# Layer 1's twelve modulation chunks as products on VectorE in dense blocks 0 to 6, identity products in their place in the second attention

## The chip, the cores and the metric

The kernel runs on one core of a Trainium2 chip. The metric is the device time of one execution in microseconds (us). Three runs of the kernel before took 1367.85, 1368.5 and 1369.38 us; the median is 1368.5 us.

## The reference, cut to what matters

A trunk of two layers works on 256 tokens of width 1024, in f32. Each layer takes six modulation vectors of 1024 numbers from a conditioning vector `c`, and uses them around an attention and around a feed-forward part: dense in layer 0, eight experts (two per token) in layer 1.

```python
c_act = silu(c)
for layer in range(2):
    mod = c_act @ ada_w[layer] + ada_b[layer]        # 1024 x 6144 weights, one row
    sh_m, sc_m, g_m, sh_f, sc_f, g_f = split(mod, 6)
    h = rms_norm(x, norm_mix_g[layer]) * (1 + sc_m) + sh_m
    x = x + g_m * token_mixer(h, ...)                # in-projection, attention, out-projection
    h = rms_norm(x, norm_ffn_g[layer]) * (1 + sc_f) + sh_f
    y = swiglu(h, ...) if layer % 2 == 0 else moe_swiglu(h, ...)
    x = x + g_f * y
return rms_norm(x, final_g)
```

The change touches only `c_act @ ada_w[1]`, a vector times a 25 MB matrix, and when and on which engine it is done.

## The kernel before, in words

**Stages.** In order of time: a lead-in with layer 0's first modulation chunks, layer 0's in-projection, first attention and out-projection, the dense feed-forward in seven blocks of 512 hidden columns (`dense`, blocks 0 to 6), layer 1's in-projection, second attention and out-projection, the router, and the experts (352 MB of weights). Each engine runs its own hand-written instruction list, tied together by semaphores. Nothing is reordered at run time.

**Weights.** SP issues nearly all weight DMAs, in one in-order queue. Up to the second out-projection weights land in five slots of 2 MB: slots 0, 1 and 2 of `W`, and two spare ones. ScalarE copies a weight slot to a rounded high part (L1010), VectorE subtracts to get the low part (L1328), and PE multiplies high by high, low by high and high by low (L2256 to L2258). A slot is free once both splits are done. A dense block takes slot 0 and 1 for gate and up weights (parts 0 to 3) and slot 2 for down weights (parts 4 and 5).

**Modulation.** `ada_w` of a layer is cut into twelve chunks of 2 MB. Four chunks (`n // 4`, a round) give 2048 of the 6144 numbers; each holds a quarter of the 1024 rows of the sum. There are two ways to work one off:

- On PE (`ada_chunk`, L2178): eight products of the conditioning column `c_rep` with 512 columns, four of them side by side in four column groups.
- On VectorE (`products`, L1653 and L1655): weight slot times a column of `vcols`, added to `ada_acc` (128 x 2048), two instructions per chunk, after which `ada_summed` is raised. The first instruction of a round overwrites `ada_acc` and is shorter. When four chunks are in, PE adds over partitions with four products by ones (`sum_rows`, L2422) and raises `ada_rows`. VectorE then adds the bias (`mod_round`, L1392).

Before, layer 0's chunks all go through PE. Of layer 1's, chunks 0 to 7 go through VectorE in dense blocks 1 to 4, two per block (`ADA_BLOCKS`): slot 1's in `before_last_units`, slot 2's in `after`. Their loads go into the weight slots between two blocks' weights, so the next block's weights for that slot wait for `ada_summed`. Chunks 8 to 11 go through PE in the second attention, one in each of its first four steps, from slots 1, 2 and the spare ones. The sums of rounds 0 and 1 stand behind the last product of blocks 2 and 4.

**Experts.** 18 buffers of 1 MB (`raw`), in pairs r = 0 to 8, lie over the memory of earlier stages, and `first_free(r)` says what must have ended before a pair is first filled: for r = 0, 1, 3 and 5 the modulation chunks 8 to 11, for the others parts of the out-projection. Later fills wait for PE to finish with what the buffer held.

The prediction also names `turned` (VectorE's low part of transposed activations, L1640), `gated` (gate times up, L1635), `turn` (PE's transposes of activations, L2388), `dense_out` (gated residual addition, L1937) and `keep` (products of the identity with itself that nobody reads, L2186).

## Time and profile before

| what | us |
|---|---|
| median of three runs | 1368.5 |
| the profiled execution, its own time | 1368.58 |
| its span on the core | 1366.8 |
| PE busy | 1296.5 |
| VectorE (DVE) busy | 452.3 |
| ScalarE (ACT) busy | 290.5 |

Dense block 0 begins at about 161 us, the in-projection of layer 1 at about 398, the second attention at 456.9 and the first expert's products at 541.25. From then to the end the experts' weights stream in.

How to read the rows: a row of a timeline has the start, the duration, engine, line, operation, output and inputs, shape and count; in brackets stands how long the engine had been idle and who ended it. A row of windows has the stretch, its length, the busy time of PE, PEld (weight load), DVE, ACT and POOL with counts, TensorE's granted clock (1.00 is 2.4 GHz, 0.50 is 1.2 GHz), the busy share of the DMA engines and GB/s. A row of the chain has start, duration, engine and line. PE shows two rows' worth of records for one f32 product of the attention, `ada_chunk`, `sum_rows` and `keep` (x8 is four products).

### The profile page before, as it was taken

What the parts mean: (1) busy time and instruction counts of PE and PEld (TensorE: products, weight loads), DVE (VectorE), ACT (ScalarE), POOL (GpSimd) and SP (SyncE); (2) the same over time, 40 slices, a digit from 0 to 9 for tenths busy, and PEclk for the clock granted to TensorE, in tenths of its full rate; (3) what the DMA queues carried; (4) which work ended last, traced back from release to release, by engine and by line L of the source; (5) the groups of instructions that cost most, each with busy time, mean ns of one, the idle gap of its engine ahead of it and who ended that gap; (6) DMA issues with size and microseconds to landing.
All of it is one profiled execution on the core that took longest, in us unless ns stands there. A gap on an engine that the chain in (4) does not pass through costs nothing.

```text
span 1366.8 us, 24966 instructions
## 1 busy us (share of the span) xinstructions
PE 1296.5 (95%) x10994; PEld 704.0 (52%) x10995; DVE 452.3 (33%) x808; ACT 290.5 (21%) x520; POOL 32.8 (2%) x82
## 2 busy tenths in 40 slices
PE   5999999999999989997689999999999999899997
PEld 4766888787888676431233333443343333243342
DVE  4876867777459665200100120001101110000011
ACT  2346544343433462110010000010010000010000
POOL 1101100000001010000000000000000000000000
PEclk9999999999999999998889999999999999899999
DMA  9989748888436758999999999999999999999996
GB/s 336 322 339 330 233 175 312 309 299 307 177 124 209 306 198 316 377 418 419 417 420 418 420 419 417 407 407 420 418 419 420 420 420 418 418 417 420 418 419 252
DMA packets 101695, 482.13 MB, mean 353 GB/s; under 512 B 9768, under 2 KB 11888, under 8 KB 67792
## 3 DMA queue, kind: packets, MB, share of 16 engines
q1 hardware_dynamic: 97632, 475.06, 86.9%
q10 hardware_dynamic: 2720, 2.93, 0.8%
q0 software_dynamic: 1232, 2.50, 0.7%
q8 instruction: 88, 1.44, 0.4%
q14 instruction: 23, 0.19, 0.0%
HBM read 477.32 MB, written 1.05 MB: 350 GB/s over the span
## 4 chain that ended last, share of the span: by engine, by line
PE 82%; DMA 8%; DVE 4%; ACT 2%; SPq 2%; issue 1%; POOL 0%; DVEq 0%; ACTq 0%
PE ps L2572 32%; PE ps L2615 15%; PE ps L2256 8%; PE ps L2258 8%; PE ps L2257 8%; DMA raw<-in_moe_w_down_dram 5%; DMA weights<-in_ada_w_dram 2%; DMA raw<-in_moe_w_up_dram 2%; PE ps L2631 1%; SPq L850 1%; PE ps L2589 1%; DVE weights_lo L1328 1%; PE ps L2546 1%; PE ps L2337 1%; PE ps L2178 1%
## 5 line engine op out<-in xcount | busy, mean ns | idle before, releaser
L2572 PE MATMUL ps<-raw,hX 128*32 128x512 f32 (+1 forms) x4864 | 478.2, 546 | 19.2 <-DMA raw<-in_moe_w_up_dram 14.3
L2572 PEld LDWEIGHTS ps<-raw,hX 128*32 128x32 f32 x4864 | 153.9, 110 | 316.5 <-issue 274.3
L2615 PE MATMUL ps<-raw,m_actT 128*32 128x512 f32 x1568 | 181.1, 606 | 1.7 <-DMA raw<-in_moe_w_down_dram 1.7
L2256 PE MATMUL ps<-weights_hi,hT_hi 128*128 128x512 f32 (+1 forms) x416 | 162.2, 390 | 2.6 <-DVE hT_lo L1434 1.4
L1749 DVE TENSOR_TENSOR m_act<-m_act,ps 128x512 f32<-128x512 f32 (+1 forms) x28 | 17.4, 621 | 432.7 <-PE ps L2572 431.9
L2258 PE MATMUL ps<-weights_hi,hT_lo 128*128 128x512 f32 (+1 forms) x416 | 159.1, 383 | 0.0
L2257 PE MATMUL ps<-weights_lo,hT_hi 128*128 128x512 f32 (+1 forms) x416 | 158.7, 382 | 0.0
L1328 DVE TENSOR_TENSOR weights_lo<-weights,weights_hi 128x2048 fp32r<-128x2048 f32 (+1 forms) x52 | 113.2, 2203 | 2.3 <-ACT weights_hi L1010 1.1
L2615 PEld LDWEIGHTS ps<-raw,m_actT 128*32 128x32 f32 x1568 | 51.6, 112 | 112.6 <-issue 100.8
L1010 ACT ACTIVATE weights_hi<-weights 128x2048 fp32r<-128x2048 f32 (+1 forms) x48 | 87.2, 1841 | 56.0 <-PE ps L2258 51.4
L2256 PEld LDWEIGHTS ps<-weights_hi,hT_hi 128*128 128x128 f32 x416 | 78.3, 188 | 20.9 <-issue 4.8
L2258 PEld LDWEIGHTS ps<-weights_hi,hT_lo 128*128 128x128 f32 x416 | 78.3, 188 | 15.6
L2257 PEld LDWEIGHTS ps<-weights_lo,hT_hi 128*128 128x128 f32 x416 | 78.4, 188 | 14.0
L2615 PE MATMUL ps<-raw,m_actTX 128*32 128x256 f32 x1120 | 73.5, 398 | 10.7 <-issue 6.1
L1190 ACT ACTIVATE m_actTX<-ps 128x512 f32<-128x512 f32 (+1 forms) x10 | 5.4, 544 | 320.4 <-PE ps L2589 320.4
L2615 PEld LDWEIGHTS ps<-raw,m_actTX 128*32 128x32 f32 x1120 | 37.4, 114 | 56.3 <-issue 34.4
L1749 DVE TENSOR_TENSOR m_actX<-m_actX,ps 128x512 f32<-128x512 f32 (+1 forms) x10 | 6.2, 621 | 170.4 <-PE ps L2572 170.2
L1185 ACT ACTIVATE m_act<-ps 128x512 f32<-128x512 f32 (+1 forms) x28 | 15.2, 544 | 168.8 <-PE ps L2572 168.8
L1190 ACT ACTIVATE m_actT<-ps 128x512 f32<-128x512 f32 (+1 forms) x28 | 13.4, 548 | 158.4 <-PE ps L2589 158.4
L2256 PE MATMUL ps<-down_hi,actT_hi 128*128 128x512 f32 x112 | 44.4, 396 | 0.0
L2258 PE MATMUL ps<-down_hi,actT_lo 128*128 128x512 f32 x112 | 43.7, 390 | 0.0
L2257 PE MATMUL ps<-down_lo,actT_hi 128*128 128x512 f32 x112 | 43.7, 390 | 0.0
(281 smaller groups left out, 1074.9 us busy)
## 6 DMA issues: line engine op xcount, KB each, us to landing
raw<-in_moe_w_down_dram SPq DMA_DIRECT2D x96, 1024.0 KB, 22.3
raw<-in_moe_w_gate_dram SPq DMA_DIRECT2D x64, 1024.0 KB, 16.9
raw<-in_moe_w_up_dram SPq DMA_DIRECT2D x64, 1024.0 KB, 23.0
raw<-in_moe_w_gate_dram SPq DMA_DIRECT2D x64, 768.0 KB, 21.6
raw<-in_moe_w_up_dram SPq DMA_DIRECT2D x64, 768.0 KB, 21.8
weights<-in_ada_w_dram SPq DMA_DIRECT2D x19, 2048.0 KB, 10.0
raw<-in_moe_w_down_dram SPq DMA_DIRECT2D x32, 512.0 KB, 20.8
weights<-in_ffn_w_gate_dram SPq DMA_DIRECT2D x14, 1024.0 KB, 5.2
```

The costliest lines, as they stand in the source:

```text
L850: sp.dma_start(raw[b][:, 0:WIDE[n]].rearrange("p (k n) -> p k n", k=1), src.rearrange("a p k n -> p (a k) n")).then_inc(sig.loaded[b], 16)
L1010: act.activation(halves(hslot)[0][:, off:off + n], W[:, wslot, off:off + n], ACT.Copy).then_inc(hi_done, 1)
L1185: act.activation(unit_act(c, b, n), unit_bank(c, b, n), ACT.Silu).then_inc(sig.silu, 1)
L1190: act.activation(unit_turned(z, c, b, n), unit_bank(c, b, n).rearrange("p (j n) -> p j n", n=P), ACT.Copy).then_inc(sig.copied, 1)
L1328: dve.tensor_tensor(lo[:, at], W[:, wslot, at], hi[:, at].bitcast(F32), ALU.subtract).then_inc(lo_done, 1)
L1749: dve.tensor_tensor(unit_act(c, b, n), unit_act(c, b, n), unit_bank(c, b, n), ALU.mult).then_inc(sig.act, 1)
L2178: mm = pe.matmul(ps[32 * g:32 * g + 32, bank, :], c_rep[:, k, :], held(slot)[:, kk * 2048 + g * 512:kk * 2048 + g * 512 + 512], start=(k = ...
L2256: pe.matmul(dst, stat_hi, hi, start=start, stop=False, skip_group_check=True)
L2257: pe.matmul(dst, stat_hi, lo, start=False, stop=False, skip_group_check=True)
L2258: return pe.matmul(dst, stat_lo, hi, start=False, stop=stop, skip_group_check=True)
L2572: mm = pe.matmul(ps[32 * q:32 * q + 32, bank, 0:COL[n]], hX[:, i, at32:at32 + 32], raw[buffer][:, at:at + COL[n]], start=(i == 0), stop=(i ...
L2615: mm = pe.matmul(ps[32 * quarter:32 * quarter + 32, bank, col:col + w], stationary[:, 32 * half:32 * half + 32], raw[buffer][:, D * j + w ...
```

## The change: what it does

All twelve chunks of layer 1 go through VectorE, in the 14 places (block, slot 1 or 2) without the first and the last: one in block 0 (slot 2), two in each of blocks 1 to 5, one in block 6 (slot 1). Chunk n therefore moves one place earlier: chunk 0 from block 1, slot 1, to block 0, slot 2, and so on. `sum_rows` runs three times, each inside its block (2, 4, 6) in front of `down(1)`. `mod_round` of round 2 moves from the second attention to block 6. `first_free` of the first eight expert buffers now waits for the in-projection alone. The second attention's first four steps get four identity products each instead of a chunk.

```diff
-ADA_LATER = [[(0, n) for n in range(ADA_FIRST, ADA_CHUNKS)], [(1, n) for n in range(8, ADA_CHUNKS)]]
-ADA_STEP = [[0, 1, 2, 3, 4, 5, 6, 7], [0, 1, 2, 3]]
-ADA_BLOCKS = (1, 2, 3, 4)
-ADA_SLOTS = (1, 2)
+ADA_LATER = [[(0, n) for n in range(ADA_FIRST, ADA_CHUNKS)], []]
+ADA_STEP = [[0, 1, 2, 3, 4, 5, 6, 7], []]
+ADA_DENSE = [(b, slot) for b in range(NB) for slot in (1, 2)][1:-1]
 def ada_of_block(b):
-    return [(2 * ADA_BLOCKS.index(b) + i, slot) for i, slot in enumerate(ADA_SLOTS)] if b in ADA_BLOCKS else []
+    return [(n, slot) for n, (a, slot) in enumerate(ADA_DENSE) if a == b]
...
+    holder[ADA_DENSE[-1][1]] = ("summed", len(ADA_DENSE))
     mixer(1, 0)
...
+                def ada_after(j):
+                    for n, slot in ada_of_block(j - 1):
+                        slot_split(slot, j)
+                        sp.dma_start(W[:, slot, :].rearrange("p (k n) -> p k n", k=2),
+                                     ada_v[1, n // 4, n % 4]).then_inc(w_loaded[slot], 16)
                 for j in range(NB):
                     for c in range(2):
                         if c == 1:
-                            for n, slot in ada_of_block(j - 1):
...
+                            ada_after(j)
...
+                ada_after(NB)
...
-                if r in (0, 1, 3, 5):
-                    sp.wait_ge(ada_used, ada_count(1, {0: 8, 1: 9, 3: 10, 5: 11}[r]))
+                if r in (0, 1):
+                    sp.wait_ge(hi_done, IN_BASE[1] + IN_PARTS + 2 * (r - 1))
+                    sp.wait_ge(lo_done, IN_BASE[1] + IN_PARTS + 2 * (r - 1))
+                elif r in (3, 5):
+                    sp.wait_ge(parts_used, IN_BASE[1] + IN_PARTS)
...
-                        if n == 4:
-                            dve.wait_ge(ada_rows, 1)
+                        if n and n % 4 == 0:
+                            dve.wait_ge(ada_rows, n // 4)
...
                 def after(b):
-                    products(b, 1)
+                    products(b, 2)
...
-                    products(b, 0)
+                    products(b, 1)
...
                 def last():
                     b = NB - 1
                     before_last_units(b)
+                    mod_round(1, 2)
...
-                pe.wait_ge(mod_ready, (1, 3, 4, 6)[n])
+                pe.wait_ge(mod_ready, (1, 3, 6, 6)[n])
...
+                    if layer and j < 4:
+                        keep(4, 2)
...
                     gate_up(2, high_k, b, is_first)
+                    if b in (2, 4):
+                        sum_rows(b // 2 - 1)
                     down(1, (0, 1), b, is_first)
...
-                    for r in range(2):
-                        if b == ADA_BLOCKS[2 * r + 1]:
-                            sum_rows(r)
...
                     gate_up(2, high_k, b, False)
+                    sum_rows(2)
                     down(1, (0, 1), b, False, True)
```

**SP's queue at dense block 1.** The gate and up loads come in pairs, slot 0's first, then slot 1's; `in_ffn_w_down` is slot 2's. Before, from slot 0 of block 1 on:

```order
L836 DMA weights<-in_ffn_w_gate_dram 128x4x512
L836 DMA weights<-in_ffn_w_up_dram 128x4x512
L836 DMA weights<-in_ffn_w_gate_dram 128x4x512
L836 DMA weights<-in_ffn_w_up_dram 128x4x512
L842 DMA weights<-in_ffn_w_down_dram 128x4x1024
```

Now:

```order
L836 DMA weights<-in_ffn_w_gate_dram 128x4x512
L836 DMA weights<-in_ffn_w_up_dram 128x4x512
L822 DMA weights<-in_ada_w_dram 128x2x2048
L836 DMA weights<-in_ffn_w_gate_dram 128x4x512
L836 DMA weights<-in_ffn_w_up_dram 128x4x512
L842 DMA weights<-in_ffn_w_down_dram 128x4x1024
```

The load of chunk 0 into slot 2 stands ahead of slot 1's gate and up weights of block 1, and waits until block 0's down weights are split.

**VectorE at the end of dense block 0.** Before, from the second down part on:

```order
L1328 TENSOR_TENSOR down_lo<-weights,down_hi 128x2048
L1640 TENSOR_TENSOR actT_lo<-ps,actT_hi 128x256
L1635 TENSOR_TENSOR act<-sg,ps 128x256
L1640 TENSOR_TENSOR actT_lo<-ps,actT_hi 128x256
L1328 TENSOR_TENSOR weights_lo<-weights,weights_hi 128x2048
L1635 TENSOR_TENSOR act<-sg,ps 128x256
```

Now:

```order
L1332 TENSOR_TENSOR down_lo<-weights,down_hi 128x2048
L1644 TENSOR_TENSOR actT_lo<-ps,actT_hi 128x256
L1639 TENSOR_TENSOR act<-sg,ps 128x256
L1659 TENSOR_SCALAR ada_acc<-weights,vcols 128x2048
L1661 SCALAR_TENSOR_TENSOR ada_acc<-weights,vcols,ada_acc 128x2048
L1644 TENSOR_TENSOR actT_lo<-ps,actT_hi 128x256
L1332 TENSOR_TENSOR weights_lo<-weights,weights_hi 128x2048
L1639 TENSOR_TENSOR act<-sg,ps 128x256
```

Chunk 0's two products stand ahead of the third unit's `turned` (the second of the `actT_lo` rows), and with it ahead of the first split of block 1's weights (`weights_lo`) and of the last `gated`.

**PE in the first four steps of the second attention.** `ps<-qkT` are scores, `ident,E` transposes of the probabilities, `v,PT` the values. Before:

```order
L2310 MATMUL ps<-qkT 128x256 x4
L2178 MATMUL ps<-weights,c_rep 32x512 x8
L2310 MATMUL ps<-qkT 128x256 x4
L2178 MATMUL ps<-weights,c_rep 32x512 x8
L2310 MATMUL ps<-qkT 128x256 x4
L2322 MATMUL ps<-ident,E 128x128 x4
L2337 MATMUL ps<-v,PT 128x128 x2
L2178 MATMUL ps<-spare_72,c_rep 32x512 x8
L2310 MATMUL ps<-qkT 128x256 x4
L2322 MATMUL ps<-ident,E 128x128 x2
L2337 MATMUL ps<-v,PT 128x128 x2
```

Now:

```order
L2317 MATMUL ps<-qkT 128x256 x4
L2193 MATMUL ps<-ident 128x128 x4
L2317 MATMUL ps<-qkT 128x256 x4
L2193 MATMUL ps<-ident 128x128 x4
L2317 MATMUL ps<-qkT 128x256 x4
L2329 MATMUL ps<-ident,E 128x128 x4
L2344 MATMUL ps<-v,PT 128x128 x2
L2193 MATMUL ps<-ident 128x128 x4
L2317 MATMUL ps<-qkT 128x256 x4
L2329 MATMUL ps<-ident,E 128x128 x2
L2344 MATMUL ps<-v,PT 128x128 x2
```

In each of the steps a chunk of eight wide products became four identity products of 128 columns.

## Rows read from the trace of the kernel before

**Rows 1.** Page, chain that ended last, shares by engine.
```profile
PE 82%; DMA 8%; DVE 4%; ACT 2%; SPq 2%; issue 1%; POOL 0%; DVEq 0%; ACTq 0%
```

**Rows 2.** Windows: dense block 5, end of second attention, experts.
```profile
345.00:360.00 15.00, 15.00 (x70) 12.33 (x69) 1.55 (x4) 3.58 (x6) 0.00 (x0) 1.00 0.29 114
...
495.00:510.00 15.00, 12.06 (x84) 10.82 (x83) 8.68 (x20) 9.93 (x25) 4.95 (x9) 1.00 0.11 30
...
600.00:615.00 15.00, 15.00 (x162) 5.53 (x158) 2.33 (x5) 0.87 (x2) 0.00 (x0) 1.00 1.01 421
```

**Rows 3.** Timeline of SP's queue: block 1's down weights; the ninth expert load.
```profile
177.21 0.37 SPq L842 DMA_DIRECT2D weights<-in_ffn_w_down_dram  x1
...
511.56 19.89 SPq L850 DMA_DIRECT2D raw<-in_moe_w_up_dram  x8
```

**Rows 4.** DMA issues between 177 and 178 us.
```profile
weights<-in_ffn_w_down_dram SPq DMA_DIRECT2D x1, 2048.0 KB, 7.7
```

**Rows 5.** Tile in_ada_w_dram, issues between 456.4 and 458 us.
```profile
L769 SPq DMA_DIRECT2D spare<-in_ada_w_dram x2: 368/415/462, 456.4 to 456.8; - x2
...
DMA to landing us min/median/max: 7.5/10.5/13.4
```

**Rows 6.** The same between 202 and 206 us, one load in slot 2.
```profile
DMA to landing us min/median/max: 10.5/10.5/10.5
```

**Rows 7.** Tile ada_acc, VectorE's products.
```profile
L1655 DVE SCALAR_TENSOR_TENSOR ada_acc<-weights,vcols,ada_acc x14: 2344/2352/2353, 210.7 to 321.6; 128x2048 f32<-128x2048 f32 x14
...
L1653 DVE TENSOR_SCALAR ada_acc<-weights,vcols x2: 1281/1284/1286, 209.3 to 276.9; 128x2048 f32<-128x2048 f32 x2
```

**Rows 8.** Timeline of VectorE, end of dense block 0.
```profile
182.26 0.42 DVE L1635 TENSOR_TENSOR act<-sg,ps 128x256 f32<-128x256 f32 x1 [2.31 <-ACT sg L1123]
...
188.19 0.42 DVE L1640 TENSOR_TENSOR actT_lo<-ps,actT_hi 128x256 fp32r<-128x256 f32 x1 [5.52 <-ACT actT_hi L1127]
...
190.73 0.41 DVE L1635 TENSOR_TENSOR act<-sg,ps 128x256 f32<-128x256 f32 x1
```

**Rows 9.** Timeline of PE: block 0's last transposes; the sums behind block 2.
```profile
191.42 0.38 PE L2388 MATMUL ps<-ident,act 128*128 128x128 f32 x2
...
263.11 0.39 PE L2257 MATMUL ps<-down_lo,actT_hi 128*128 128x512 f32 x1
263.33 0.39 PE L2258 MATMUL ps<-down_hi,actT_lo 128*128 128x512 f32 x1
263.65 1.06 PE L2422 MATMUL ps<-ada_acc,ones 128*32 128x512 f32 x8
...
264.98 0.39 PE L2257 MATMUL ps<-weights_lo,hT_hi 128*128 128x512 f32 x1
```

**Rows 10.** Timeline of VectorE, dense block 6.
```profile
379.26 0.42 DVE L1635 TENSOR_TENSOR act<-sg,ps 128x256 f32<-128x256 f32 x1 [2.32 <-ACT sg L1123]
...
384.92 0.42 DVE L1640 TENSOR_TENSOR actT_lo<-ps,actT_hi 128x256 fp32r<-128x256 f32 x1 [5.24 <-ACT actT_hi L1127]
...
390.04 0.69 DVE L1937 TENSOR_TENSOR tmp_row<-ps,gate 128x512 f32<-128x512 f32 x1 [1.95 <-PE ps L2258]
```

**Rows 11.** Chain in order of time, second attention.
```profile
471.66 1.85 PE ps L2178 x16
...
476.37 1.85 PE ps L2178 x16
...
479.91 0.61 ACT PT L1092
...
500.59 1.17 PE ps L2186 x10
```

**Rows 12.** Timeline of ScalarE, second attention, around its transposed probabilities.
```profile
474.32 0.21 ACT L1104 ACTIVATE sinke<-sinkm 128x4 f32<-128x4 f32 x1
474.99 0.38 ACT L1092 ACTIVATE PT<-ps 128x256 f32<-128x256 f32 x1 [0.45 <-PE ps L2322]
...
479.36 0.21 ACT L1104 ACTIVATE sinke<-sinkm 128x4 f32<-128x4 f32 x1
```

More of the change, by code:

```diff
@@ L60 @@
 ADA_FIRST = 4
-ADA_LATER = [[(0, n) for n in range(ADA_FIRST, ADA_CHUNKS)], [(1, n) for n in range(8, ADA_CHUNKS)]]
-ADA_STEP = [[0, 1, 2, 3, 4, 5, 6, 7], [0, 1, 2, 3]]
-ADA_BLOCKS = (1, 2, 3, 4)
-ADA_SLOTS = (1, 2)
+ADA_LATER = [[(0, n) for n in range(ADA_FIRST, ADA_CHUNKS)], []]
+ADA_STEP = [[0, 1, 2, 3, 4, 5, 6, 7], []]
+ADA_DENSE = [(b, slot) for b in range(NB) for slot in (1, 2)][1:-1]
 def ada_of_block(b):
-    return [(2 * ADA_BLOCKS.index(b) + i, slot) for i, slot in enumerate(ADA_SLOTS)] if b in ADA_BLOCKS else []
-def ada_count(layer, n):
-    return ADA_CHUNKS + n - 8 + 1 if layer else n + 1
+    return [(n, slot) for n, (a, slot) in enumerate(ADA_DENSE) if a == b]
 def ada_loads_before(slot, b):
-    return 16 * sum(a < b for a in ADA_BLOCKS) if slot in ADA_SLOTS else 0
+    return 16 * sum(a < b for a, of in ADA_DENSE if of == slot)
 IN_PARTS, OUT_PARTS = 2 * IN_CHUNKS, 2 * OUT_CHUNKS
@@ L371, in mixer @@
         for slot, (of, n) in zip((one, two) + SPARE + (one, two, last, SPARE[0]), ADA_LATER[layer]):
-            put(("ada", of, n), slot, ("ada", ada_count(of, n)))
+            put(("ada", of, n), slot, ("ada", n + 1))
         put(("out", layer, 1), RING - 1, ("split", OUT_BASE[layer] + 4))
@@ L382, in plan_ring @@
     for c, dmas in enumerate((2, 2, 1)):
-        for b in ADA_BLOCKS:
+        for b in range(NB):
             for n, slot in ada_of_block(b):
@@ L759, in free @@
                     sp.wait_ge(ada_used, value)
+                elif what == "summed":
+                    sp.wait_ge(ada_summed, value)
                 elif what == "parts":
@@ L824, in dense @@
                         if c == 1:
-                            for n, slot in ada_of_block(j - 1):
-                                slot_split(slot, j)
-                                sp.dma_start(W[:, slot, :].rearrange("p (k n) -> p k n", k=2),
-                                             ada_v[1, n // 4, n % 4]).then_inc(w_loaded[slot], 16)
+                            ada_after(j)
                         before = [n for n, slot in ada_of_block(j - 1) if slot == c]
@@ L1385, in mod_round @@
             def mod_round(layer, r):
-                if layer and r < 2:
+                if layer:
                     dve.wait_ge(ada_rows, r + 1)
                 else:
-                    dve.wait_ge(ada_used, ada_count(layer, 4 * r + 3))
+                    dve.wait_ge(ada_used, 4 * r + 4)
                 dve.wait_ge(bias_loaded, 192 if layer else 64)
-                bank = 7 if layer and r < 2 else 2
+                bank = 7 if layer else 2
                 dve.tensor_tensor(modrow[:, r, :], ps[:, bank, :], modrow[:, r, :], ALU.add).then_inc(mod_ready, 1)
@@ L1641, in turned, with products @@
                                       aTh[:, i % 2, :, :].bitcast(F32), ALU.subtract).then_inc(at_lo, 1)
-                def products(b, at):
-                    for n, slot in ada_of_block(b)[at:at + 1]:
+                def products(b, of):
+                    for n, slot in ada_of_block(b):
+                        if slot != of:
+                            continue
                         dve.wait_ge(w_loaded[slot], plan[("ada", 1, n)][2])
-                        if n == 4:
-                            dve.wait_ge(ada_rows, 1)
+                        if n and n % 4 == 0:
+                            dve.wait_ge(ada_rows, n // 4)
                         for kk in range(2):
@@ L1691, in before_last_units @@
                     for r in range(2):
-                        if b == ADA_BLOCKS[2 * r + 1] + 1:
+                        if b == 2 * r + 3:
                             mod_round(1, r)
                     gated(b, 1)
-                    products(b, 0)
+                    products(b, 1)
                     turned(b, 1)
```

## The prediction, made before the changed kernel ran

> **What bounds the kernel now.** I read the chain of waits first, then windows over the stages, then the timelines of the engines where the change edits them. The chain is 82% PE and 8% DMA [rows 1]. The windows split that into stages with different limits [rows 2]. In dense block 5 PE is busy for all 15.00 of 15.00 us, while VectorE works for 1.55 and the DMA engines run at 0.29: the dense part is PE's, and one PE instruction more costs its full time. At the end of the second attention PE is busy for 12.06 of 15 us and waits in turn on ScalarE and VectorE, with DMA at 0.11: a chain of latencies. In the experts DMA runs at 1.01 and 421 GB/s, so there the end is set by bytes, counted from the moment when the stream starts.
>
> That moment decides what the freed loads are worth. SP issues the expert loads after the first eight only at 511.56 us [rows 3], when the out-projection gives up memory, and in the 15 us before it the DMA engines moved 30 GB/s [rows 2]. They were idle for want of room, not of time. The first eight buffers were full by then; filling them sooner starts no later load sooner. So the change counts by how far it shifts PE in the dense blocks and in the attention, and the experts inherit the sum of the shifts.
>
> **Dense blocks: the third sum.** Rounds 0 and 1 had a `sum_rows`, and round 2 gets one. One costs PE this: from the ordinary product at 263.33 to the second one after the sums at 264.98 are 1.65 us, of which two ordinary steps of 0.22 to 0.23 (263.11 to 263.33) make 0.46, leaving 1.2 us [rows 9]. The two old ones only change place by part of a block, 0. The new one waits for chunk 11's products. These start behind the `gated` of 379.26, take two times 2.35 us [rows 7] and end at about 384.4, just before `turned` at 384.92 [rows 10], which PE's next instruction waited for anyway. So the sum adds no wait, and costs 1.2 us.
>
> **Dense block 0: the new product.** Chunk 0's load can be issued when block 0's down weights are split, which is when SP issued block 1's down weights: 177.21 us [rows 3]. That load, alone on the queues, landed 7.7 us later [rows 4]. Chunk 0's has slot 1's two loads right behind it. The nearest pattern are two loads issued 0.4 us apart: the first landed after 7.5, the second after 13.4 us [rows 5]. The other end is 10.5 us, for a chunk load issued with the one before it still under way [rows 6]. I take 7.7 us, since nothing runs ahead of chunk 0's: it lands at 184.9. VectorE is free from the `gated` of 182.26 on, so the landing sets the start. The first product of a round takes 1.28, the second 2.35 us [rows 7], the end is 184.9 + 3.65 = 188.55. `turned` stood at 188.19 [rows 8], so VectorE is 0.4 us late there, and in the split and the `gated` of 190.73 behind it. This one ended at 191.15, and PE's `turn` took it up at 191.42 [rows 9]. Of 0.4 us, 0.3 thus reach PE. The term is 0.3 us; its bounds are 0 (landing at 7.5 and the margins a little wider) and, at 10.5 us, the product ends at 191.35: `turned` and the weights' split come 3.2 us late, and PE loses about 3.0. What is queued behind chunk 0's products is the split of block 1's parts, PE's first need in that block; its down weights go out at 188.6 instead of 177.2 and land near 196.4, early enough for a split that blocks 2 to 5 do in the same pattern today.
>
> The Trainium skill bears on the choice between 7.7 and 10.5 us (DMA: Bandwidth & Descriptors, section on queues, rings and completion order): on each DMA engine descriptors are taken in ring order, and a semaphore's increment lands after all earlier writes of that engine. By it what is queued behind does not delay a load and what is ahead does, which is the order that the two landings show [rows 5, 6]. By the rule the term stays at 0.3 us; sharing with the loads behind would make it 3.0.
>
> **Dense blocks 1 to 5.** Each holds two chunks. Blocks 1 to 4 did before, with PE at full share, and block 5 has the room (VectorE 1.55 of 15 us [rows 2]). At chunks 4 and 8 VectorE waits for `ada_rows`, but PE's sums end within some tenths of the `gated` that VectorE does first anyway, and a round's first product is 1.1 us shorter (1.28 against 2.35 [rows 7]). I take 0 for both; if the cover fails, 0.3 us each.
>
> **Block 6 and the in-projection.** `mod_round` of round 2, an operation on 128x512 like the one at 390.04 with its 0.69 us, now stands in front of that one, which had 1.95 us of idle time before it and waited for PE [rows 10]. PE arrives there 1.2 us later, so it is covered: 0. The loads of in-projection chunks 1 and 2 go out after chunk 11's products, at 384.4. With 13.4 us for the second of such a pair [rows 5] both are there by 398, before the in-projection needs them: 0. What follows moves by the 1.2 + 0.3 us as a whole.
>
> **Second attention.** A chunk costs PE 1.85 us, and the chain runs through it in steps 2 and 3 (471.66, 476.37); ten records of `keep` took 1.17 us, so eight take 0.94 [rows 11]. Each step loses 0.91 us. In steps 0 and 1 PE only gets ahead of a VectorE that is held by weight splits: 0. In step 2 the next scores come 0.91 sooner. The following copy of ScalarE, at 474.99, was idle for only 0.45 us, since the exponentials and the last small operation at 474.32 fill it [rows 12], so step 3 starts 0.4 sooner. With its own 0.91 less, the scores of step 4 come 1.3 sooner and ScalarE's copy at 479.91 [rows 11] 1.2 sooner, because ScalarE's work ahead of it moves by 0.9 and ended at 479.36 + 0.21, 0.34 us before it [rows 12]. From step 4 on nothing changed, and the shift of 1.2 us stays. Its bounds: 0.4, if only ScalarE's gap counts, and 3.6 (four times 0.91), if every step paid. That `mod_round` leaves VectorE saves nothing: it stood in idle time.
>
> **The sum.** 1368.58 us (span 1366.8 and 1.8 around it) + 1.2 + 0.3 - 1.2 = 1368.9. The profiled execution stands 0.1 above the median of the runs, so I forecast 1368.8 us: no change that can be measured. About 0.2%, 2.7 us, is what a measurement of this kernel can tell from none. The terms' bounds give 1368.5 + 1.2 + 0 - 3.6 = 1366.1 to 1368.5 + 1.2 + 3.0 - 0.4 = 1372.3.
>
> **Rivals.**
>
> *The freed DMA time is worth something (faster).* Four loads of 2.1 MB leave the stretch between in-projection and experts; at 421 GB/s [rows 2] 8.4 MB are 20 us, giving 1349 us. For it: the experts are bound by bytes. Against it: the bytes have only moved within the kernel, ahead of a stretch of DMA at 0.11 [rows 2] that no load could use. It would need the stream at 511.56 to start early, and its releases aren't touched. 4%. Other gains, such as the whole 3.6 us of the attention with a margin elsewhere on top: 3%.
>
> *Block 0's load comes late (slower).* One mechanism: chunk 0's data is behind its time, and VectorE holds `turned`, the split and `gated` behind its wait. Each us of landing beyond 7.7 costs PE about one. It is slower from 10.2 us on; at 10.5 [rows 6] the time is 1368.8 - 0.3 + 3.0 = 1371.5, at 13.4 [rows 5] 1374.4. For it: the wait is in the middle of an engine's list, with 0.4 us of margin already used up. Against it: the queues are empty at 177.2. 14%, together with similar delays in block 6.
>
> *The clock falls in the attention (slower).* The chunks' wide products go, and their substitutes take half the time. If TensorE fell from 2.4 to 1.2 GHz, its work would take twice as long. At PE's share of 12.06 in 15 us [rows 2] the first four steps (16 us) hold 13 us of it and the 43 us from first scores to out-projection 35, of which I put half on the path that sets the end: 6 to 17 us more, so 1375 to 1386 us. Against it: the stretch from 495 to 510 us has no chunk in it, PE busy for 12.06 of 15 us in scores, transposes and values, and a granted clock of 1.00 [rows 2]. 3%.
>
> The Trainium skill speaks for this rival (TensorE: Matmul & The Clock Gate, parts 1 and 4): activity releases the throttle, an idle stretch brings half rate back, and transposes do not count as activity in the same way. By it, what is left of steps 0 to 3 would be poor in activity, and the 1375 us above would be its result. The same mix without chunks at full clock in the row above is why I give it little.
>
> **Chances.** The forecast with its bounds 76%, the late load 14%, the clock 3%, freed DMA or more 7%. Faster by over 0.2%: 7%. Within 0.2%: 77% (the forecast, and a load that is late by under 2.5 us). Slower by over 0.2%: 16%. The range is 1366.3 to 1372.0 us; it leaves out the 20 us gain, the clock and the worse half of the late load.
>
> **What would show it.** Chunk 0's first product near 184.9 us, block 0's last `turn` at about 191.7 and block 1's first product 0.3 us later than before; the third sum near 387 with 1.2 us around it; layer 1's in-projection and the attention's first scores 1.5 us later than before; the attention from first scores to out-projection 1.2 us shorter; first expert products at 541.5, SP's ninth expert load at 511.8; clock 1.00 from 460 to 510. The forecast is wrong if the first expert products come before 538.6 or after 544, or if the time from there to the end, 825.5 us of the span, changes by more than 1 us. It is wrong in its reasons if the two shifts are absent and only their sum is right.

## The result: 4.3 us slower, and the profile after

| | kernel before | kernel after |
|---|---|---|
| median of 20 runs each, taken side by side, us | 1369.36 | 1373.69 |
| the runs | 1367.85 to 1372.78 | 1368.86 to 1375.69, and one of 3045.27 |
| the profiled execution, its own time / span | 1368.58 / 1366.8 | 1374.36 / 1372.5 |
| first scores of the second attention | 462.28 | 464.15 |
| start of its out-projection | 505.38 | 510.09 |
| first expert products | 541.25 | 545.96 |
| from there to the end of the span | 825.55 | 826.54 |

The ratio is 1.0022 [1.0014, 1.0031]: slower by what a measurement can just tell, and the median is outside the range of the prediction. The ratio leaves out the execution of 3045.27; without it the median is 1373.53. The 20 times are not spread evenly. Six lie from 1368.86 to 1370.64, where the kernel before lies; thirteen from 1373.03 to 1375.69; between them is nothing.

The profiled execution has three places where the time went: 1.87 us up to the first scores (forecast 1.5), 2.84 us in the attention (forecast 1.2 less), 0.99 us in the experts (forecast 0). The chain's shares by engine, against [rows 1]: PE 80% for 82%, DMA 12% for 8%.

```profile
PE 80%; DMA 12%; DVE 5%; ACT 2%; issue 1%; SPq 1%; POOL 0%; DVEq 0%; ACTq 0%
```

Windows of the kernel after, first the three of [rows 2], then short ones:

```profile
345.00:360.00 15.00, 15.00 (x70) 12.35 (x69) 10.59 (x7) 3.00 (x5) 0.00 (x0) 1.00 0.76 287
495.00:510.00 15.00, 11.90 (x78) 11.34 (x77) 6.32 (x17) 8.10 (x28) 0.14 (x1) 0.77 0.01 1
600.00:615.00 15.00, 15.00 (x176) 5.16 (x172) 2.33 (x5) 0.00 (x0) 0.00 (x0) 1.00 1.02 424
...
471.00:474.00 3.00, 1.75 (x11) 1.54 (x12) 2.93 (x5) 1.93 (x8) 0.00 (x0) 0.86 1.01 386
474.00:477.00 3.00, 3.00 (x15) 2.30 (x14) 1.51 (x6) 2.03 (x9) 0.00 (x0) 0.57 1.10 431
501.00:504.00 3.00, 2.80 (x13) 2.83 (x14) 0.29 (x1) 1.73 (x6) 0.00 (x0) 0.50 0.00 0
504.00:507.00 3.00, 3.00 (x16) 3.00 (x16) 0.00 (x0) 1.05 (x8) 0.00 (x0) 0.50 0.00 0
585.00:588.00 3.00, 3.00 (x25) 1.59 (x28) 0.00 (x0) 2.05 (x8) 0.00 (x0) 0.64 1.03 424
```

The third number from the right is the granted clock. In dense block 5 it is 1.00, with VectorE now at 10.59 us for 1.55. In the attention it falls to 1.2 GHz at two places, around 474 and from 501 to 507 us, and once more in the experts. In the kernel before's trace no window from 456 to 624 us shows less than 1.00. Behind that, from about 630 us on, the clock falls in every trace of this document, the kernel before's too. This is the kernel before, in ten microseconds in which PE waits 5.4 us for weights, at a clock of 0.70:

```profile
630.00:640.00 10.00, 6.03 (x36) 0.77 (x32) 0.00 (x0) 0.00 (x0) 0.00 (x0) 0.70 1.01 422
```

So "no fall" below always means: none from 456 to 624 us. The window of 495 to 510, which the prediction took as its evidence, has 0.77 for 1.00, though its instructions are the same. DMA is at 0.01 there: no other load used the time that the four loads gave back. SP's ninth expert load followed the out-projection, from 511.56 [rows 3] to:

```profile
516.53 0.80 SPq L851 DMA_DIRECT2D raw<-in_moe_w_up_dram  x2
```

The chain of the kernel after in the attention (start, duration, engine, output, line), against [rows 11]:

```profile
473.75 1.71 PE ps L2193 x8
475.46 1.64 PE ps L2317 x8
...
478.89 0.89 PE ps L2193 x8
479.79 1.09 PE ps L2317 x8
...
501.20 1.09 PE ps L2329 x4
502.29 1.60 PE ps L2344 x8
503.89 2.24 PE ps L2193 x10
```

L2193 is `keep`, L2317 the scores. The same eight records take 1.71 us in one step and 0.89 in the next, the scores 1.64 and 1.09. The ten old identity records at 503.89 take 2.24 us where they took 1.17 [rows 11].

The dense part is as the prediction had it. VectorE at the end of block 0 and PE's `turn`, against [rows 8] and [rows 9]:

```profile
184.86 1.29 DVE L1659 TENSOR_SCALAR ada_acc<-weights,vcols 128x2048 f32<-128x2048 f32 x1 [2.09 <-DMA weights<-in_ada_w_dram]
186.18 2.35 DVE L1661 SCALAR_TENSOR_TENSOR ada_acc<-weights,vcols,ada_acc 128x2048 f32<-128x2048 f32 x1
188.57 0.42 DVE L1644 TENSOR_TENSOR actT_lo<-ps,actT_hi 128x256 fp32r<-128x256 f32 x1
```

```profile
191.57 0.44 PE L2397 MATMUL ps<-ident,act 128*128 128x128 f32 x2
```

The third sum on PE, and VectorE behind it in block 6, against [rows 9] and [rows 10]:

```profile
387.49 0.39 PE L2265 MATMUL ps<-weights_hi,hT_lo 128*128 128x512 f32 x1
387.81 1.06 PE L2431 MATMUL ps<-ada_acc,ones 128*32 128x512 f32 x8
388.81 0.50 PE L2263 MATMUL ps<-down_hi,actT_hi 128*128 128x512 f32 x1
```

```profile
388.94 0.69 DVE L1396 TENSOR_TENSOR modrow<-ps,modrow 128x512 f32<-128x512 f32 x1 [0.19 <-PE ps L2431]
391.93 0.69 DVE L1944 TENSOR_TENSOR tmp_row<-ps,gate 128x512 f32<-128x512 f32 x1 [2.30 <-PE ps L2265]
```

`tmp_row` had 1.95 us of idle time before it and has 2.30 now: the moved `mod_round` is covered.

### The profile page after: what moved, and what is told of

Same layout as the page of the kernel before. It is cut to its first block, busy times and chain, and to the rows that moved or that the text cites. A ratio compares the mean times of both kernels' runs of the same rounds, so it can differ in the third digit from the quotient of the medians.

```text
span 1372.5 us, 24933 instructions
## 1 busy us (share of the span) xinstructions
PE 1300.5 (95%) x10970; PEld 708.2 (52%) x10971; DVE 470.3 (34%) x816; ACT 290.9 (21%) x520; POOL 32.9 (2%) x82
## 3 DMA queue, kind: packets, MB, share of 16 engines
q8 instruction: 88, 1.44, 0.4%
## 4 chain that ended last, share of the span: by engine, by line
PE 80%; DMA 12%; DVE 5%; ACT 2%; issue 1%; SPq 1%; POOL 0%; DVEq 0%; ACTq 0%
PE ps L2580 31%; PE ps L2623 14%; DMA raw<-in_moe_w_down_dram 10%; PE ps L2263 8%; PE ps L2265 8%; PE ps L2264 8%; DMA weights<-in_ada_w_dram 2%; PE ps L2639 1%; PE ps L2597 1%; DVE weights_lo L1332 1%; PE ps L2554 1%; PE ps L2344 1%; DVE mx L1537 1%; PE ps L2317 1%; PE ps L2329 1%
## 5 line engine op out<-in xcount | busy, mean ns | idle before, releaser
L1661 DVE SCALAR_TENSOR_TENSOR ada_acc<-weights,vcols,ada_acc 128x2048 f32<-128x2048 f32 x21 | 49.4, 2350 | 3.0 <-DMA weights<-in_ada_w_dram 2.5
```

Of the source, the lines that this page charges most:

```text
L1661: a = dve.scalar_tensor_tensor(out=ada_acc[:], in0=w, scalar=c, in1=ada_acc[:], op0=ALU.mult, op1=ALU.add)
```

## The experiments

In each, "scores" and "out-projection" are the first instruction of each on PE, "attention" the time between them (43.10 us in the kernel before's trace), "rest" the span from the first expert products on (825.55). "High" counts the executions over 1371.7 us: in the largest set of the kernel before nothing lies between 1370.63 and 1371.74, and of its 126 executions in all sets 16 are higher (10 of them in that largest set of 35, 6 in the other 91). The counts take in the executions of 1671.99, 1674.51 and 3045.27 us. A kernel that is delayed by work of its own passes 1371.7 sooner. Most runs have one trace each, so a fall that it shows is one execution's.

**1. The kernel after, again**, and what stands in the chunks' place. `e2_nokeep` leaves the four identity products per step out. `e3_wide` puts eight unread products of the chunk's own shape there, so that PE's list in the attention is as before and only the loads are gone.

```diff
 # e2_nokeep
-                    if layer and j < 4:
-                        keep(4, 2)
 # e3_wide
-                        keep(4, 2)
+                        for kk in range(2):
+                            for g in range(4):
+                                pe.matmul(ps[32 * g:32 * g + 32, 2, :], c_rep[:, kk, :], fing[:, 0:512], start=True, stop=True)
```

> The changed kernel once more, for a second trace and more times. The clock theory: the granted clock falls to 1.2 GHz in the second attention in some executions and not in others, each fall there costs PE 1.5 to 2.5 us, and the times fall into two groups, near 1369.3 (no fall) and near 1374 us. If this trace has no stretch of clock below 0.9 between 456 and 520 us, its own time is under 1371 us and the first expert products start near 542 us; if it has falls as in the first trace, they start 3 to 5 us later. The late-load rival: the clock has nothing to do with it, and the time lost shows in the dense blocks (first scores later than 464.5 us in slow executions).

> The changed kernel without the four identity products in each of the first four steps of the second attention. The clock theory: less PE work between 464 and 480 us, so the clock falls there in most executions, median 1373 to 1377 us, at least as slow as the changed kernel. The rival that PE's time is all that counts: up to 1.9 us less in the attention, so 1368 to 1372 us and faster than the changed kernel.

> The changed kernel with eight products of 32 x 512 (the shape of a modulation chunk, on data that lies there, result unused) in place of the four identity products of each of the four steps. PE's list in the attention is then that of the kernel before, while the loads, the dense blocks and the third sum are those of the changed kernel. The clock theory: no falls, 1.8 us for the sums and block 0, no gain in the attention: 1370.3 us (1369.8 to 1371), faster than the changed kernel though PE has 3.7 us more to do. The rival that something in loads or dense blocks makes the loss: it stays at 1373 to 1375 us. If the freed DMA time were worth anything, it would be under 1368.5.

| | median, ratio | high | attention | clock under 1.00 |
|---|---|---|---|---|
| e1_again | 1374.36, 1.0031 [1.002, 1.0043] | 6 of 8 | 45.84 | 471–477, 498–507, 585–591 |
| e2_nokeep | 1373.11, 1.0022 [1.0012, 1.0032] | 6 of 8 | 45.47 | 468–477, 498–507, 585–591 |
| e3_wide | 1373.14, 1.0023 [1.0013, 1.0032] | 6 of 10 | 45.81 | 498–507, 585–591 |

The result repeats, though the times of `e1_again` are not two clean groups: 1371.3 and 1371.71 lie between. `e2_nokeep` is where the clock theory put it (1373 to 1377). The narrow products neither cause the fall at 498 nor prevent the one at 471. With the wide ones the early fall (471 to 477 us) is gone and the late one (498 to 507) isn't:

```profile
471.00:474.00 3.00, 2.22 (x20) 1.29 (x24) 2.88 (x6) 1.54 (x7) 0.00 (x0) 1.00 1.05 406
...
501.00:504.00 3.00, 3.00 (x16) 3.00 (x16) 0.00 (x0) 2.33 (x10) 0.00 (x0) 0.50 0.03 5
```

The expectation for it (no fall, 1370.3) failed. The early fall stands in all five traces in which the wide products are gone and nothing else fills the stretch (the kernel after four times, `e2_nokeep`), so it comes of what took the chunks' place. The late one doesn't.

**2. Filling the sparse stretch.** Identity products nobody reads go ahead of PE's waits on the probabilities, first too many, then fewer.

```diff
 # e4_fill (e5_fit: 6, 4, 6 in steps 2, 7, 8, and 3, 3, 4 in steps 4, 5, 8)
+                    if layer and j in (2, 7, 8):
+                        keep({2: 10, 7: 8, 8: 10}[j], 2)
                     if 0 <= a < UNITS:
                         turn_probs(a)
                     if a >= 2:
                         values(a - 1)
+                    if layer and j in (5, 6, 8):
+                        keep(6, 2)
```

> The changed kernel with more identity products in the second attention, put where PE waits anyway: ten, six, six, eight, ten and six of them ahead of transposes of probabilities in steps 2, 5, 6, 7 and 8 (in step 8 before both). The clock theory: PE's waits of 0.8 to 1.7 us there are filled, the clock stays at 2.4 GHz, and the gain of 1.2 us in the attention shows: 1369.2 us (1368.7 to 1370.5). The rival that identity products don't hold the clock: 1373 to 1375 us as the changed kernel. If they don't fit in the waits: each of them that is late adds 0.1 us, at most 3 us.

> The changed kernel with further identity products that fit into PE's waits (0.23 us each): six ahead of the first transposes of step 2, three ahead of the second transposes of steps 4 and 5, four ahead of the first of step 7, six and four in step 8. The run with more of them held the clock but cost 2.6 us, since they were sized at half of what one costs. The clock theory: no fall between 456 and 520 us, and next to none of the cost: 1369.3 us (1368.9 to 1370.5), all times in one group within 1.5 us. The rival that only an overfull PE list holds the clock: falls come back, median over 1372 us.

`e4_fill`: 1372.59, 1.0024 [1.0015, 1.0032], 9 of 11 high, attention 44.54, no fall anywhere up to 624 us. I had read one product as half of what it costs: ten, as 20 records, took 2.50 us.

```profile
469.57 2.50 PE L2193 MATMUL ps<-ident 128*128 128x128 f32 x20
```

`e5_fit`: 1370.36, 0.9997 [0.9988, 1.0007], 2 of 12 high. Scores at 463.70, attention 41.73: at full clock the forecast's 1.2 us are there, and a little more. The times spread over 3.4 us, though, where 1.5 had been expected. The clock falls in the experts' second gather, and DMA from 585 to 588 us moves 252 GB/s, where it was 391 in the kernel before (rest 828.93):

```profile
501.00:504.00 3.00, 2.89 (x28) 2.78 (x27) 0.87 (x2) 2.19 (x11) 0.00 (x0) 1.00 0.00 0
...
582.00:585.00 3.00, 3.00 (x24) 0.90 (x20) 0.00 (x0) 2.06 (x8) 0.00 (x0) 0.50 0.91 368
585.00:588.00 3.00, 3.00 (x28) 0.92 (x24) 0.00 (x0) 0.00 (x0) 0.00 (x0) 0.61 0.87 252
```

Against the kernel after, this is the same change with waits in steps 2, 4, 5, 7 and 8 filled; its trace has no fall in the attention, and its median is 3.3 us lower. The ratio to the kernel before flatters it a little: 10 of that kernel's 35 executions in this set are high, and against their median it stands 0.8 us above.

**3. Delay or loads?** Three theories of the late fall: PE reaches it later (the third sum), the missing DMA traffic, chance. `e6_sum3` gives the kernel before only a third sum, `e7_shift3` 13 identity products in its place, `e8_loads` keeps the dense part of after and has the attention load and multiply its four chunks again (unread; the first expert buffers wait for them as in the kernel before).

```diff
 # e6_sum3, on the kernel before, block 6
+                    pe.wait_ge(mod_ready, 5)
+                    for g in range(4):
+                        pe.matmul(ps[32 * g:32 * g + 32, 7, :], ones[:, 0:32], ada_acc[:, 512 * g:512 * g + 512], start=True, stop=True)
 # e7_shift3, same place
+                    pe.wait_ge(mod_ready, 5)
+                    keep(13, 7)
 # e8_loads, on the kernel after
-ADA_LATER = [[(0, n) for n in range(ADA_FIRST, ADA_CHUNKS)], []]
-ADA_STEP = [[0, 1, 2, 3, 4, 5, 6, 7], []]
+ADA_LATER = [[(0, n) for n in range(ADA_FIRST, ADA_CHUNKS)], [(2, n) for n in range(8, ADA_CHUNKS)]]
+ADA_STEP = [[0, 1, 2, 3, 4, 5, 6, 7], [0, 1, 2, 3]]
...
-                    if layer and j < 4:
-                        keep(4, 2)
```

> The kernel before with four products by ones in block 6 (the third sum's, on what lies in ada_acc, result unused) and nothing else. It moves all that follows by 1.2 us, and leaves the loads, the chunks in the attention and VectorE alone. The position theory (whether the clock falls after the sparse stretch at the end of the attention depends on when in the execution it comes): slow executions near 1374 us appear as with the changed kernel, in a third or more. The load theory (the clock falls since the DMA engines are idle from 486 us on, where the kernel before loads until 494): none, all near 1370.3 us.

> The kernel before with 13 identity products (3.0 us) at the same place in block 6. The sum alone: 1372.1 us. The position theory: another share of executions with a fall than for 1.2 us, either few (all within 1.5 us of 1372.1) or most (near 1376). The load theory: no falls, 1372.1.

> The changed kernel with the second attention of the kernel before: chunks 8 to 11 are loaded there once more and multiplied on PE in steps 0 to 3 (result unused), and the first eight expert buffers wait for that. It differs from the run with eight wide products per step in the DMA traffic alone. The load theory: no falls, all times near 1370.3 us. The position theory: two groups as with the wide products, near 1370 and 1374.5, median over 1372.

| | median, ratio | high | scores | attention | clock under 1.00 |
|---|---|---|---|---|---|
| e6_sum3 | 1371.28, 1.001 [0.9998, 1.0021] | 5 of 12 | 463.46 | 44.55 | 498–507 |
| e7_shift3 | 1372.05, 1.002 [1.001, 1.0031] | 7 of 12 | 464.67 | 44.55 | 501–507 |
| e8_loads | 1372.0, 1.0013 [1.0, 1.0026] | 7 of 12 | 463.56 | 45.82 | 498–507, 585–591 |

All three show the late fall in their one trace. In `e8_loads` PE is at half clock from 501 on after DMA at 1.03 in the same attention, so the missing traffic isn't what it takes:

```profile
486.00:489.00 3.00, 2.19 (x20) 2.05 (x20) 1.54 (x6) 2.19 (x9) 1.04 (x1) 1.00 1.03 423
...
501.00:504.00 3.00, 3.00 (x16) 3.00 (x15) 0.00 (x0) 2.47 (x10) 0.00 (x0) 0.50 0.02 5
```

And in `e6_sum3` the kernel before falls once it is 1.18 us late:

```profile
501.00:504.00 3.00, 3.00 (x16) 3.00 (x16) 0.00 (x0) 2.72 (x11) 0.00 (x0) 0.50 0.02 5
```

The medians are less clear. `e6_sum3` is 1.7 us above its set's 1369.56 where its delay is 1.2; `e7_shift3` 2.5 where its delay is 2.4, though its lowest is 3.6 above the lowest of before (1371.37, 1367.73), and its own delay lifts executions over 1371.7. Nor do the counts speak for the delay. With the limit raised by each kernel's delay, 3 of 12 are high in `e6_sum3` and 2 of 12 in `e7_shift3`, against 10 of 35 in the kernel before of the same set; the traced execution of `e6_sum3`, which has the fall, just misses the raised limit (1372.85 for 1372.9). In the traces the delay goes with the fall; that it makes the fall more frequent is not shown.

**4. One kernel, two executions.**

> The changed kernel, another look. With a fall in the attention: first expert products 3 to 5 us later than without, own time over 1373 us. Without: clock 1.00 from 456 to 520 us, attention 1.2 us shorter than before, first expert products near 542 us, own time under 1371.

> The same once more: with a fall in the attention over 1373 us, without one under 1371 us. If a look without falls takes 1373 or more, or one with them under 1371, the clock theory falls.

Both are the kernel after, unchanged, one execution each: 1375.56 and 1370.48 us, one of either group. This pair shows the cause best, since nothing differs but the execution. Windows of `e11_look`:

```profile
471.00:474.00 3.00, 2.23 (x12) 2.02 (x13) 2.87 (x6) 1.54 (x7) 0.00 (x0) 0.75 1.05 405
501.00:504.00 3.00, 3.00 (x16) 3.00 (x15) 0.00 (x0) 2.17 (x8) 0.00 (x0) 0.50 0.00 0
504.00:507.00 3.00, 3.00 (x18) 3.00 (x17) 0.00 (x0) 1.03 (x5) 0.00 (x0) 0.56 0.00 0
...
585.00:588.00 3.00, 3.00 (x23) 1.17 (x26) 0.00 (x0) 2.26 (x8) 0.00 (x0) 0.52 1.00 412
```

and of `e12_look`:

```profile
471.00:474.00 3.00, 2.44 (x13) 2.24 (x12) 2.83 (x7) 1.56 (x7) 0.00 (x0) 0.50 1.04 406
501.00:504.00 3.00, 2.89 (x27) 2.78 (x27) 0.15 (x1) 2.78 (x12) 0.00 (x0) 1.00 0.00 0
504.00:507.00 3.00, 3.00 (x24) 2.87 (x25) 2.17 (x7) 2.41 (x3) 1.38 (x2) 1.00 0.02 5
...
585.00:588.00 3.00, 3.00 (x43) 1.17 (x36) 0.00 (x0) 0.00 (x0) 0.00 (x0) 1.00 0.95 372
```

The ten old identity records, first of `e11_look`, then of `e12_look` (count, busy us and mean ns, idle):

```profile
L2193 PE MATMUL ps<-ident 128*128 128x128 f32 x10 | 2.4, 432 | 0.0
```

```profile
L2193 PE MATMUL ps<-ident 128*128 128x128 f32 x10 | 1.3, 280 | 0.0
```

The second execution has no fall from 477 to 624 us. Its attention takes 42.91 us, the first's 45.81. To split the 2.90 us I take the first transposes of step 8, at the start of the stretch in which the clock falls late, first of `e12_look`, then of `e11_look`:

```profile
497.55 0.66 PE L2329 MATMUL ps<-ident,E 128*128 128x128 f32 x4 [1.58 <-DVE rec L1555]
```

```profile
498.37 0.66 PE L2329 MATMUL ps<-ident,E 128*128 128x128 f32 x4 [1.57 <-DVE rec L1555]
```

From there to the out-projection are 8.60 us in the one and 11.13 in the other: the late fall costs 2.5 us. From the scores to there are 34.31 and 34.68, and 33.13 in `e5_fit`, which has no fall (and other fill): the early one costs about 1.2 and 1.5. The rest is 828.35 and 826.58, 1.8 us more in the execution with a fall in the gather. How much of that is the fall's is open: the rest is 825.55 to 827.22 us in the traces without a fall and without extra work in the gather, and 826.54 to 828.93 in those with one. Together 2.9, 1.8 and the 0.45 by which the scores of `e11_look` come later make the difference of the spans, 1373.7 and 1368.6.

The expectation said that a fall in the attention under 1371 us would refute the clock theory. `e12_look` is such a case, with half clock from 471 to 474. It refutes the theory as it was put, with each fall alike; what separates these two times is the late fall and what follows, not the early one.

**5. Repairing.** `e9_gather` is `e5_fit` with four 256-column products between those of the experts' second gather. `e10_old_fit` gives the kernel before the same fill there and in steps 5, 7 and 8 (with PE's wait for `mod_ready` moved up to step 5, ahead of the first write to that bank), `e14_old_steps` in the steps alone.

```diff
 # e9_gather, e10_old_fit: the gather
+                    if sig is main and count == 2 and k % 2:
+                        pe.matmul(ps[:, banks[0], 256:512], ident[:], xn[:, 0, 0:256], start=True, stop=True)
 # e10_old_fit, e14_old_steps: the attention of the kernel before
+                    if layer and j in (7, 8):
+                        keep({7: 4, 8: 6}[j], 2)
...
+                    if layer and j in (5, 8):
+                        keep(4 if j == 8 else 3, 2)
```

> The changed kernel with the fitting identity products, and four products of 256 columns between those of the expert stage's second gather (32 products of 32 columns, about 3.6 us), after whose start the clock fell in five of the seven traces of changed kernels that I have. The clock theory: no fall in the attention and none at the gather; the four products cost 1 us of PE, a fall there 1.5 to 3 us of the time that follows. Median 1369.6 us (1369.0 to 1370.4), spread under 2 us; the fitting products alone had 1370.4 and 1368.7 to 1372.1. The rival that the falls in the experts cost nothing, since the stage is bound by DMA: 1 us or 0 slower than with the fitting products alone, with the same spread.

> The kernel before (four chunks on PE in the second attention, two sums) with the fitting identity products in steps 5, 7 and 8 and the four in the gather. The clock theory: the slower group of the kernel before (about a third of its times lie above 1371.5 us) goes, and all times are within 1367.9 and 1370 us, median 1368.8, faster than the kernel before by 0.3 to 1 us and than every version with three sums. The rival: no effect on the groups, median 1369.5 or, with the gather's 1 us, 1370.5.

> The kernel before with the fitting identity products in steps 5, 7 and 8 of the second attention, and nothing in the experts' gather, whose four products cost 1.7 us there. The clock theory: no falls in the attention, so no times over 1372.5 us; falls in the experts stay possible. Median 1369.0 us, the same as before or up to 0.5 us faster, and faster than every version with three sums. The rival (identity products take more than they keep): 1369.8 or more.

| | median, ratio | high | attention | rest | falls |
|---|---|---|---|---|---|
| e9_gather | 1371.31, 1.0017 [1.0008, 1.0026] | 5 of 11, up to 1372.46 | 41.71 | 827.89 | none |
| e10_old_fit | 1370.87, 1.0011 [1.0002, 1.002] | 1 of 11 | 43.09 | 828.61 | none |
| e14_old_steps | 1369.65, 1.0002 [0.9993, 1.001] | 0 of 11 | 43.08 | 826.07 | none |

The gather's four cost 1.73 us in `e9_gather` (from its start to the next product 5.31 us for 3.58 in the kernel before), more than the 1.0 I had priced, and both kernels with them lose. The median of `e9_gather` is 0.95 us above that of `e5_fit`, which is also what the rival of its expectation said (a fall in the gather costs nothing); the two are from different sets. (That expectation counts a fall there in five of seven traces; it is six, all but `e4_fill`.) The steps' fill on the kernel before costs nothing and its eleven executions end at 1370.87, but the median isn't lower, and 0 high of 11 against 2 of 23 may be chance. No version beats the kernel before.

**6. Without the third sum.** `e13_no_third` is `e8_loads` without the sum in block 6: round 2 comes from the chunks in the attention, as before.

```diff
 # e13_no_third, further to e8_loads
-                    mod_round(1, 2)
...
-                    sum_rows(2)
```

> The kernel of the run e8 (changed dense blocks, chunks 8 to 11 loaded and multiplied once more in the second attention) without the third sum: round 2 is taken from the attention's products as in the kernel before, while VectorE still works off all twelve chunks in the dense blocks. What follows block 6 is then 0.5 us later than before instead of 1.8. The position theory: the share of executions with a fall goes back towards the kernel before's (about one in six), median 1369.3 to 1370 us. The rival that VectorE's products or the loads in blocks 0, 5 and 6 bring the falls: as e8, half of the times above 1371.5 us.

> The kernel before, another look. Without a fall from 456 to 520 us its own time is under 1370.5 us and the first expert products start near 541.3. With one, they start near 544 and its time is over 1371.5.

`e13_no_third`: 1369.62, 1.0008 [0.9998, 1.0017], 3 of 12 high, scores at 462.12, attention 43.08, no fall in its trace. Against `e8_loads` this is 2.4 us less, with scores 1.44 us earlier, but the two intervals overlap and 3 in 12 against 7 in 12 may be chance. `e15_look`, one more execution of the kernel before (1370.5 us), has falls too, at other places, and its span is 1.9 us longer than that of the trace that the prediction read. Its expectation failed: with a fall in the attention it was to take over 1371.5 us and start the experts near 544; it started them at 541.93.

```profile
486.00:489.00 3.00, 3.00 (x19) 2.13 (x18) 0.41 (x3) 2.42 (x9) 1.04 (x1) 0.66 1.03 423
489.00:492.00 3.00, 3.00 (x22) 2.83 (x22) 2.86 (x6) 1.05 (x3) 0.00 (x0) 0.77 0.99 412
...
582.00:585.00 3.00, 3.00 (x24) 0.93 (x20) 0.00 (x0) 2.20 (x8) 0.00 (x0) 0.59 1.00 407
```

**7. The traces put in order.** One thing in the traces does tell the executions apart: when PE reaches the first transposes of step 8. This sorts all twelve that have no further fill:

| first transposes of step 8, us | late fall | from there to the out-projection |
|---|---|---|
| 496.61 `e13_no_third`, 496.78 before, 497.47 `e15_look`, 497.55 `e12_look` | no | 8.59 to 8.60 |
| 497.96 `e6_sum3`, 499.17 `e7_shift3` | yes | 10.05 |
| 497.58 `e2_nokeep`, 498.06 `e8_loads`, 498.17 `e1_again`, 498.20 `e3_wide`, 498.37 `e11_look`, 498.86 after | yes | 11.13 to 11.49 |

PE's two waits in step 8 are the same, 1.6 us for VectorE and 1.2 for ScalarE, in `e12_look` and in `e11_look`. So `e11_look` differs from `e12_look` in being 0.82 us later at that place, 0.45 of it there at the scores and 0.37 by an early fall that costs more. By this order an early fall, which costs over a microsecond, moves a kernel towards the late one. With the waits filled, lateness alone brings no fall: `e4_fill` gets there at 499.96 and keeps 1.00. The order was found afterwards, most kernels have one trace in it, and its two sides are only 0.03 us apart. It says that lateness goes with the fall, not what in it matters.

## Why the prediction was wrong, step by step

**The third sum, 1.2 us: right.** The shift of PE's instructions rises by 1.24 us there, and nothing waits.

**Block 0, 0.3 us: right in place, 0.13 in size.** Chunk 0's load landed for a product at 184.86, forecast 184.9; `turned` is 0.38 us late, and the block costs PE 0.13: its `turn` stands at 191.57 for 191.42, and the next block's instructions are 0.22 late, of which 0.09 was there before block 0. The load had slot 1's two loads right behind it and landed as the lone one of [rows 4]. The rule of the Trainium skill that the prediction drew on (DMA: Bandwidth & Descriptors, queues, rings and completion order), that each DMA engine takes descriptors in ring order, agrees with this landing, which what was queued behind did not delay. The rival of the late load fell with it.

**Old sums "only change place, 0": wrong by a little.** Inside blocks 2 and 4 a sum takes 1.24 us from PE, behind the block it took 1.07: twice 0.17 us. Together that is 0.09 + 0.13 + 0.34 + 1.24 = 1.8 us at the in-projection. The forecast had 1.5. The four traces of the kernel after have their first scores 0.96 to 1.87 us later than 462.28, so the difference is within what executions differ by. Blocks 1 to 5 and `mod_round` cost nothing, as said.

**Freed DMA time worth nothing: right.** No expert load came earlier; with the traffic gone and PE's list kept (`e3_wide`) no execution was under 1369.74 us, where a gain was to show as under 1368.5.

**Attention, 1.2 us shorter: the right mechanism under a clock that isn't granted.** `e5_fit` shows 1.4 us at full clock, though with other fill in it. One identity set takes PE 0.98 to 1.09 us at full clock, from its start to the next instruction's, for 0.94. In three of the four traces of the kernel after the attention is 2.7 to 2.8 us longer instead, in the fourth, with the early fall alone, 0.2 shorter.

**The step that failed** is the one that gave the rival "the clock falls in the attention" 3%: "the stretch from 495 to 510 us has no chunk in it, PE busy for 12.06 of 15 us [...] and a granted clock of 1.00". The row was read as a property of these instructions. It was that of one execution. The prediction named two limits for its own failure: first expert products after 544 us, which came (545.96), and a rest changed by more than 1 us, which just did not (0.99). In the kernel after, the same instructions are granted 1.00 in one execution and 0.50 in the next, and the kernel before itself falls in some. The rule of the Trainium skill set beside it (TensorE: Matmul & The Clock Gate, part 1), that activity releases the throttle and an idle stretch brings half rate back, was the better guide for the early fall, which came where wide products had gone and stayed away when they were back. It stayed away as well where six or ten narrow products filled PE's wait in step 2 (`e4_fill`, `e5_fit`, `e9_gather`). For the late one the rule names no more than a candidate: PE waits for ScalarE and VectorE there in every kernel, and no instruction differs between `e11_look` and `e12_look`. The rival's price was too high as well, 6 to 17 us, since it took the half clock for four steps or the whole attention. It lasts some 3 to 7 us at a place and costs 1.2 to 1.6 us early and 2.5 to 2.9 late (1.45 in `e6_sum3` and `e7_shift3`), and at most 1.8 in the gather, whose falls the prediction had not considered, where "the experts inherit the sum of the shifts" left no room for one.

**What stays open.** Why the late fall is frequent in the kernel after (14 of 20 executions high) and rare before (16 of 126, 10 of them in one set of 35). A later arrival goes with it in every trace without further fill, but medians leave only 0.5 us for it in `e6_sum3` (1.7 less the delay of 1.2) and the counts there are no higher than the kernel before's. In the kernel after they leave 3.9 (4.3 less the 0.4 that 1.8 of delay and 1.4 of shorter attention make); the early and the late fall of its trace make 1.6 and 2.6. Whether the missing traffic adds to it is not settled either: `e3_wide` (1.0023) and `e8_loads` (1.0013) have overlapping intervals. Nor is it known whether the fall in the gather follows from that in the attention: `e5_fit` has it alone, `e6_sum3` has only the other.

## What to carry to other kernels

A granted clock of 1.00 in one trace speaks for one execution: where PE's chain has waits in it, look at several traces, and at whether the times fall into groups, before you count on it. A stage that is cleared of work is also cleared of what kept PE busy: here its own products then took up to twice their time. That a delay in one stage is paid for in a later one is what the order of the traces suggests; it is not proven. The five traces with unread products in PE's waits keep 1.00 in the attention, but only what fits into the wait is free: size them by their measured duration, 0.25 us for a 128 x 128 f32 identity product in such a wait here.

## What was not expected of the hardware

- Ten identity records of one kernel in one place took 1.3 and 2.4 us, by the execution alone.
- Once PE is at 1.2 GHz in the experts' gather, the stream suffers as well: 252 GB/s for 391 in three microseconds of `e5_fit`. SP waits for PE's products to free a buffer, and issues the next loads at 584.54 us for 582.70. PE's lateness seems to count, by whatever cause: `e9_gather`, at 1.00 but with four products more in the gather, moves 305 GB/s in the same window.
- Three executions stand far outside, 3045.27 us (after), 1671.99 (before) and 1674.51 (`e8_loads`). They have no trace, and nothing explains them.
